# Loading each block of the second expert table as two 64-partition DMAs, one begun by SyncE and one by ScalarE

## The chip, the cores and the metric

The kernel runs on one core of one Trainium2 chip. Its engines are TensorE (PE), VectorE (DVE), ScalarE (ACT), GpSimd (POOL) and SyncE (SP); SP computes nothing here and begins DMAs. ACT and POOL also begin DMAs, and the profile shows the transfers of SP on queue q1, those of ACT on queue q10 and those of POOL on queue q0. All of them are carried by the core's 16 DMA engines. The metric is the device time of one execution in microseconds; shorter is better.

## The reference, cut to what matters

One layer of a hybrid encoder on 384 tokens (256 of a prompt, 128 of running streams), all in float32:

```
proj = rmsnorm(x) @ w_in                     # pool branch, q, k, v
h = x + concat(pool_mixer, diff_attention) @ w_out
xn = rmsnorm(h)
# PEER: 8 heads choose 16 of 16384 experts for each token
s = (xn @ w_pq) against sub_keys;  eidx, g = the 16 best of 128 x 128 pairs, softmax over them
a = gelu(u_tab[eidx] . xn)                   # u_tab is 16384 x 2048 float32, 134 MB
y = h + sum_k (g * a)[k] * v_tab[eidx[k]]    # v_tab is 16384 x 2048 float32, 134 MB
```

The outputs are y and the new keys, values and pooling rows. The change touches only the last line: how v_tab comes into the chip.

## The kernel before, in words

The layer is computed in stages. In the profiled execution the projections, attention and the output product fill the first 660 us, the query product and the search for the best keys most of what comes before 860 us, the stage of the first table (u) runs from there to about 1870 us, and the stage of the second table (v) from there to the end.

**The v stage.** v_tab is read once and whole, as 128 blocks of 128 experts (`v_v`, line 299: partition p of block m holds row 128 p + m, which is 8 KB). For the first 256 tokens y is a dense product: for each block, TensorE multiplies a 128 x 256 matrix of weights (gate times activation, mostly zero) with the 128 x 2048 block. A float32 product of full precision is made of three: each operand is split in a rounded part "hi" and a rest "lo", and `three` (lines 1296 to 1299) issues hi.hi, hi.lo, lo.hi. A block is 24 matmuls of 128 x 512 (`v_step`). The sums stay in the eight PSUM banks through all blocks.

For each block m the steps are:

- SP loads the block, 1 MB, into one of four buffers `vraw[m % 4]` (`v_weights`, line 375), once the lo part of block m - 4 has been made from that buffer (the wait on `lo_done` at line 412).
- ACT waits for the block (`v_in`) and writes its hi part, `v_hi`, line 814. After the even blocks it also writes the hi part of the weights of two blocks, `w_hi`, line 819.
- DVE writes the lo part, line 1257, and signals `lo_done`. After the lo part of an even block it multiplies the gates and activations of two blocks (`w_product`, line 1221), after that of an odd block it writes the lo part of the weights (`w_lo`, line 1226), for which it waits on the `w_hi` that ACT issues behind the hi part of the next, even block.
- SP also loads the dense gates and activations, 2 times 256 KB for two blocks (`v_routes`, line 379), on the same queue.

The names `v_raw` and `raw` in the profile are the buffers of blocks 0 and 1 and of blocks 2 and 3 (modulo 4); their hi parts are `ring_hi` and `v_hi`, their lo parts `ring_lo` and `v_lo`.

Beside this, the last 128 tokens are done without the product. For each of their 128 choices, POOL gathers the 128 rows of v_tab that the tokens chose, 1 MB in 8 KB rows, into one of five buffers (`gather_row`, line 529), and DVE adds them into `h` with their weights (`add_row`, line 1240). POOL waits with a gather until DVE has used the row that lay in its buffer. Before every eighth row POOL also gathers 8 columns of activations, one number a partition (`gather_gelus`, line 537). These adds stand in DVE's program between the lo parts, about 1.05 of them a block.

Every engine follows its own program in the order written; nothing is scheduled at run time. A wait in ACT's program holds up all that ACT does behind it.

**The u stage**, which is not changed, matters because it moves its blocks in a similar way: each 1 MB block of u_tab comes in eight DMAs of 32 partitions with runs of 2 KB (`u_piece`, line 301). SP begins the four pieces of partitions 0 to 31 and 64 to 95 (line 349), ACT the four of partitions 96 to 127 and 32 to 63 (`u_upper`, line 774). Before that, the w_pq blocks come in four pieces of 32 partitions, all from SP (line 344), while w_in and w_out blocks come in four DMAs of 128 partitions (line 327). All of these have runs of 2 KB.

Of the kernel before, what the change touches and what calls it, by code (L numbers as in the profile page):

```python
# [21 lines left out]
P = 128  # L22
# [24 lines left out]
BASE_V = BASE_U + P  # L47
# [32 lines left out]
VS = 4  # L80
# [41 lines left out]
def hybrid_layer(nc, I, O):  # L122
    F32, F32R, U32 = mybir.dt.float32, mybir.dt.float32r, mybir.dt.uint32
    ALU, ACT, AX = mybir.AluOpType, mybir.ActivationFunctionType, mybir.AxisListType
    ds = bass.ds
    ctx = ExitStack()
    with ctx:
# [6 lines left out]
        def at(name, kb, shape, dt=F32):  # L134
            return nc.alloc_sbuf_tensor_at(name, shape, dt, offset=base + int(kb * KB))
# [100 lines left out]
        vraw = [at("v_raw0", WK + 32, [P, D])[:, :], at("v_raw1", WK + 40, [P, D])[:, :], raw[:, 0, :], raw[:, 1, :]]  # L236
# [15 lines left out]
        def sem(n):  # L252
            names[n] = ctx.enter_context(nc.semaphore(n))
            return names[n]
# [5 lines left out]
        hi_done, lo_done, split_used = sem("hi_done"), sem("lo_done"), sem("split_used")  # L260
# [21 lines left out]
        v_in = [sem(f"v_in{i}") for i in range(VS)]  # L282
# [16 lines left out]
        v_v = I["v_tab"][0].rearrange("(p q) d -> p q d", q=P)  # L299

        def u_piece(m, k, a, h):

            return (raw[32 * a:32 * a + 32, k, 2 * h * W:2 * (h + 1) * W].rearrange("p (q r d) -> p q r d", r=2, q=1),
                    u_v[a, :, ds(m, 1), 2 * h:2 * h + 2, :])

        def wait_block(eng, t, blk, n_last):

            if t < NT - 1:
                eng.wait_ge(proj_ready, blk * 2 + (t + 1))
            else:  # L310
                eng.wait_ge(split_used, n_last + 3)
# [7 lines left out]
        def _(sp):  # L319
# [36 lines left out]
            def stored_gelu(mp, k):  # L356

                sp.wait_ge(a_store[k], mp * 16 + 16)
                sp.sem_inc(a_free, 1)
# [14 lines left out]

            def v_weights(m, slot):

                sp.dma_start(vraw[slot], v_v[:, ds(m, 1), :].rearrange("p o d -> p (o d)")).then_inc(v_in[slot], 16)

            def v_routes(j, par):

                sp.dma_start(gt[:, par, :, :], Gd[ds(j * 2, 2), :, :].rearrange("q p t -> p q t")).then_inc(ag_in[par], 16)
                sp.dma_start(at_[:, par, :, :], Ad[ds(j * 2, 2), :, 0:TD].rearrange("q p t -> p q t")).then_inc(ag_in[par], 16)

            sp.wait_ge(rt_ready, NT)
            v_weights(0, 0)
            v_weights(1, 1)
            sp.wait_ge(dot_done, DOTS)
            stored_gelu(P // 2 - 3, 1)
            store_gelu(P - 4, 0)
# [3 lines left out]
            v_routes(0, 0)  # L393
            sp.wait_ge(u_turn, P + 1)
            v_weights(2, 2)
            sp.wait_ge(u_turn, P + 2)
            v_weights(3, 3)
            v_routes(1, 1)
            stored_gelu(P // 2 - 2, 1)
            store_gelu(P - 2, 0)  # L400
# [5 lines left out]
            with sp.Fori(1, P // VS) as it:  # L406
                for par in range(2):
                    sp.wait_ge(w_mult, it * 2 + (par - 1))
                    v_routes(it * 2 + par, par)
                    for q in range(2):  # L410
                        s = 2 * par + q
# [150 lines left out]
        def _(act):  # L562
# [50 lines left out]
            with act.Fori(0, NG) as g:  # L613
                def evac_block(blk, tiles=range(NT)):
                    dst = qk[:, blk, :, :] if blk < 2 else vs[:, :, :]
                    for t in tiles:
                        wait_block(act, t, g * 3 + blk, g * 12 + (4 * blk + 3))
                        A(dst[:, t, :], bank[t][:, :], ACT.Copy).then_inc(proj_free, 1)

                for s in range(SPLIT, 12):  # L620
                    split_hi(g * 12 + s, s % 2)
                    m = s // 4 - 1
# [97 lines left out]
            for t in range(NT):  # L720
                wait_block(act, t, 9, BASE_POOL + 3)
                A(ptok[:, t, :], bank[t][:, :], ACT.Copy).then_inc(proj_free, 1)
# [90 lines left out]

            def v_hi(m, s, sets):

                act.wait_ge(v_in[s], sets * 16 + 16)
                A(vH[s], vraw[s], ACT.Copy).then_inc(hi_done, 1)

            def w_hi(j, par):

                act.wait_ge(w_mult, j + 1)
                A(wth[:, par, :, :], wt[:, par, :, :], ACT.Copy).then_inc(wh_done, 1)

            act.wait_ge(split_used, BASE_V + 1)
            v_hi(0, 0, 0)
            w_hi(0, 0)
            act.wait_ge(split_used, BASE_V + 2)
            v_hi(1, 1, 0)
            v_hi(2, 2, 0)
            w_hi(1, 1)  # L830
            v_hi(3, 3, 0)
            with act.Fori(1, P // VS) as it:
                for s in range(VS):
                    act.wait_ge(split_used, it * VS + (s + BASE_V - 1))
                    v_hi(it * VS + s, s, it)
                    if s % 2 == 0:
                        act.wait_ge(split_used, it * VS + (s + BASE_V))
                        w_hi(it * 2 + s // 2, s // 2)


        @block.vector
        def _(dve):
# [241 lines left out]
            def add_residual(nb, tiles=range(NT)):  # L1084
                for t in tiles:
                    wait_block(dve, t, 10 + nb, BASE_WOUT + 4 * nb + 3)
                    hs = hh[:, t, nb * W:(nb + 1) * W]
                    V.tensor_tensor(hs, bank[t][:, :], hs, ALU.add).then_inc(h_done, 1)
# [496 lines left out]
```

## Time and profile before

| | us |
|---|---|
| median of 3 runs | 2655.49 (2642.95 to 2659.84) |
| the profiled execution, its own time | 2656.08 |
| its span, first to last instruction | 2654.5 |
| PE busy | 2437.1 (92% of the span) |
| DVE busy | 1922.1 (72%) |
| POOL busy | 1171.8 (44%) |
| ACT busy | 932.1 (35%) |

How the rows below are read. A row of **windows** gives the stretch in us from the span's start and its length, the busy us and instruction counts of PE, PE's weight loads, DVE, ACT and POOL, then TensorE's granted clock as a share of full speed, the busy share of the 16 DMA engines, and GB/s moved. An answer on the **DMAs** of a stretch has packets, MB and mean rate; then for each queue its packets, its MB, and the time of its packets as a share of 16 engines times the stretch; then the issues, with the KB of each and the median us from issue to landing. Its row GB/s cuts the stretch in 40 equal slices. A **waits** row reads: who waited, for whom, us in all, how often, the longest. A **timeline** row has start, duration (both us), engine, line and operation, and in brackets the idle time before and what ended it. A row of a **tile** or a line gives counts, the least, median and longest duration in ns, and the first and last start in us.

### The profile page before, as it was taken

What the parts mean: (1) busy time and instruction counts of PE and PEld (TensorE: products, weight loads), DVE (VectorE), ACT (ScalarE), POOL (GpSimd) and SP (SyncE); (2) the same over time, 40 slices, a digit from 0 to 9 for tenths busy, and PEclk for the clock granted to TensorE, in tenths of its full rate; (3) what the DMA queues carried; (4) which work ended last, traced back from release to release, by engine and by line L of the source; (5) the groups of instructions that cost most, each with busy time, mean ns of one, the idle gap of its engine ahead of it and who ended that gap; (6) DMA issues with size and microseconds to landing.
All of it is one profiled execution on the core that took longest, in us unless ns stands there. A gap on an engine that the chain in (4) does not pass through costs nothing.

```text
span 2654.5 us, 38865 instructions
## 1 busy us (share of the span) xinstructions
PE 2437.1 (92%) x13838; PEld 2178.1 (82%) x13838; DVE 1922.1 (72%) x2105; ACT 932.1 (35%) x1018; POOL 1171.8 (44%) x684
## 2 busy tenths in 40 slices
PE   5989999999799999999979898898998999999899
PEld 4878777788699999999979898898776777777777
DVE  4554654643567998989877776776588898888888
ACT  3354544522333333323322232222333333333333
POOL 1020101020000010177888888882676675767662
PEclk9999999999899999999989999998999999999999
DMA  5453544495355568689888998997899999999997
GB/s 184 132 186 112 174 129 135 150 380 190 81 119 122 163 199 224 183 230 220 212 235 231 264 245 231 237 241 202 304 390 390 399 385 411 387 391 406 394 398 301
DMA packets 280169, 661.43 MB, mean 249 GB/s; under 512 B 73145, under 2 KB 123129, under 8 KB 237912
## 3 DMA queue, kind: packets, MB, share of 16 engines
q1 hardware_dynamic: 154832, 334.57, 38.9%
q0 software_dynamic: 82064, 249.26, 27.7%
q10 hardware_dynamic: 43191, 76.58, 10.2%
q8 instruction: 43, 0.70, 0.1%
q14 instruction: 39, 0.31, 0.0%
HBM read 613.65 MB, written 46.02 MB: 249 GB/s over the span
## 4 chain that ended last, share of the span: by engine, by line
PE 36%; POOL 25%; DMA 15%; DVE 13%; issue 7%; DVEq 1%; ACT 1%; ACTq 1%; SPq 0%; POOLq 0%
POOL g_dense L500 16%; PE banks L1297 11%; PE banks L1298 11%; PE banks L1299 11%; POOL a_values L542 6%; DMA a_tile<-a_dense 4%; DVE h L1249 4%; DMA v_row<-in_v_tab,route_place 3%; DMA raw<-in_v_tab 3%; POOL u_row L494 2%; DMA v_raw<-in_v_tab 2%; DMA raw<-in_u_tab 2%; POOL v_row L533 1%; DVEq L847 1%; DVE u_turned L1126 1%
## 5 line engine op out<-in xcount | busy, mean ns | idle before, releaser
L1297 PE MATMUL banks<-xT_hi,ring_hi 128*128 128x320 f32 (+1 forms) x2304 | 737.2, 320 | 88.4 <-DVE ring_lo L1130 81.2
L1298 PE MATMUL banks<-xT_lo,ring_hi 128*128 128x320 f32 (+1 forms) x2304 | 731.3, 317 | 0.0
L1299 PE MATMUL banks<-xT_hi,ring_lo 128*128 128x320 f32 (+1 forms) x2304 | 730.8, 317 | 0.0
L500 POOL DMA_INDIRECT g_dense<-route,route_place x256 | 497.1, 1942 | 132.1 <-issue 76.2
L1297 PEld LDWEIGHTS banks<-xT_hi,ring_hi 128*128 128x128 f32 x2304 | 444.8, 193 | 98.6 <-issue 83.3
L1298 PEld LDWEIGHTS banks<-xT_lo,ring_hi 128*128 128x128 f32 x2304 | 444.9, 193 | 0.0
L1299 PEld LDWEIGHTS banks<-xT_hi,ring_lo 128*128 128x128 f32 x2304 | 444.1, 193 | 0.0
L533 POOL DMA_INDIRECT v_row<-in_v_tab,route_place x128 | 284.4, 2222 | 187.3 <-DVE h L1249 165.4
L868 DVE TENSOR_TENSOR ring_lo<-raw,ring_hi 128x2048 fp32r<-128x2048 f32 x72 | 164.8, 2292 | 252.7 <-ACT ring_hi L580 252.4
L1130 DVE TENSOR_TENSOR ring_lo<-u_turned,ring_hi 128x2048 fp32r<-128x2048 f32 x128 | 290.5, 2270 | 72.3 <-ACT ring_hi L785 71.8
L1126 DVE STREAM_TRANSPOSE u_turned<-raw 128x2048 f32<-128x2048 f32 x128 | 295.6, 2310 | 63.7 <-DMA raw<-in_u_tab 55.5
L1249 DVE SCALAR_TENSOR_TENSOR h<-v_row,w_values,h 128x2048 f32<-128x2048 f32 x128 | 300.5, 2348 | 38.8 <-DMA v_row<-in_v_tab,route_place 36.1
L785 ACT ACTIVATE ring_hi<-u_turned 128x2048 fp32r<-128x2048 f32 x128 | 245.3, 1916 | 233.5 <-issue 220.7
L542 POOL DMA_INDIRECT a_values<-a_dense,route_place x128 | 232.5, 1817 | 60.6 <-issue 38.7
L1297 PE MATMUL banks<-v_hi,w_hi 128*128 128x512 f32 x512 | 204.3, 399 | 30.2 <-DVE v_lo L1257 30.1
L1297 PE MATMUL banks<-ring_hi,w_hi 128*128 128x512 f32 x512 | 205.1, 401 | 27.6 <-DVE ring_lo L1257 27.4
L791 ACT ACTIVATE gelu_out<-banks 128x320 f32<-128x320 f32 x128 | 56.0, 437 | 494.9 <-PE banks L1299 494.9
L580 ACT ACTIVATE ring_hi<-raw 128x2048 fp32r<-128x2048 f32 x72 | 137.6, 1914 | 214.3 <-PE banks L1299 167.0
L1298 PE MATMUL banks<-ring_lo,w_hi 128*128 128x512 f32 x512 | 203.0, 397 | 0.0
L1299 PE MATMUL banks<-ring_hi,w_lo 128*128 128x512 f32 x512 | 202.9, 396 | 0.0
L1298 PE MATMUL banks<-v_lo,w_hi 128*128 128x512 f32 x512 | 201.9, 394 | 0.0
L1299 PE MATMUL banks<-v_hi,w_lo 128*128 128x512 f32 x512 | 201.6, 394 | 0.0
(219 smaller groups left out, 3791.6 us busy)
## 6 DMA issues: line engine op xcount, KB each, us to landing
raw<-in_u_tab SPq DMA_DIRECT2D x512, 128.0 KB
raw<-in_u_tab ACTq DMA_DIRECT2D x512, 128.0 KB
v_raw<-in_v_tab SPq DMA_DIRECT2D x64, 1024.0 KB, 10.8
raw<-in_v_tab SPq DMA_DIRECT2D x64, 1024.0 KB, 12.1
raw<-in_w_in SPq DMA_DIRECT2D x160, 256.0 KB
a_dense<-gelu_out SPq DMA_DIRECT2D x128, 160.0 KB
raw<-in_w_out SPq DMA_DIRECT2D x64, 256.0 KB
g_dense<-zeros POOLq DMA_DIRECT2D x16, 1024.0 KB, 28.9
```

Of the source, the lines that this page charges most:

```text
L500: pool.indirect_dma_start(out=places, out_offset=bass.IndirectOffsetOnAxis(ap=routeU[:, t, 2, j:j + 1], axis=0), in_=route[:, t, 0, j:j + ...
L533: pool.indirect_dma_start(out=vrow[k % NVB][:, :], out_offset=None, in_=rows, in_offset=bass.IndirectOffsetOnAxis(ap=routeU[:, NT - 1, 1, ...
L542: pool.indirect_dma_start(out=aval[0:P - GT, k:k + 1], out_offset=None, in_=gelus, in_offset=bass.IndirectOffsetOnAxis(ap=routeU[0:P - GT, ...
L580: A(ringH[:, slot, :], raw[:, slot, :], ACT.Copy).then_inc(hi_done, 1)
L785: A(ringH[:, k, :].rearrange("p (b r i) -> p r b i", b=KC, r=4), uT[:, k, :].rearrange("p (r b i) -> p r b i", r=4, b=KC), ACT.Copy).then_ ...
L868: V.tensor_tensor(ringL[:, slot, :], raw[:, slot, :], ringH[:, slot, :].bitcast(F32), ALU.subtract).then_inc(lo_done, 1)
L1126: V.transpose(uT[:, k, :], raw[:, k, :]).then_inc(u_turn, 1)
L1130: V.tensor_tensor(ringL[:, k, :].rearrange("p (b r i) -> p r b i", b=KC, r=4), uT[:, k, :].rearrange("p (r b i) -> p r b i", r=4, b=KC), r ...
L1249: V.scalar_tensor_tensor(out=acc, in0=vrow[k % NVB][:, :], scalar=wval[:, k:k + 1], in1=acc, op0=ALU.mult, op1=ALU.add).then_inc(row_used, 1)
L1297: MM(out, h1, h2, start=first, stop=False)
L1298: MM(out, h1, l2, start=False, stop=False)
L1299: return MM(out, l1, h2, start=False, stop=last)
```

## The change

Each block of v_tab is loaded by two DMAs, partitions 0 to 63 and partitions 64 to 127, each 512 KB in 64 rows of 8 KB. `v_half` names the two sides.

- For blocks 0 to 3 SP begins both halves, one behind the other.
- For blocks 4 to 127 SP begins the lower half where it began the whole block, under the same wait. ACT begins the upper half of block m + 3 right behind the hi part of block m (`v_next`), and waits before it for the same count of `lo_done` as SP: the lo part of block m - 1.
- The hi part waits for both halves (the count for one set of four buffers is 32 in place of 16).
- The loop on ACT is the same otherwise; its last turn is written out, because only block 127 is left to load there.

```
+        def v_half(m, slot, half):
+            part = slice(64 * half, 64 * half + 64)
+            return vraw[slot][part, :], v_v[part, ds(m, 1), :].rearrange("p o d -> p (o d)")
...
             def v_weights(m, slot):
-                sp.dma_start(vraw[slot], v_v[:, ds(m, 1), :].rearrange("p o d -> p (o d)")).then_inc(v_in[slot], 16)
+                sp.dma_start(*v_half(m, slot, 0)).then_inc(v_in[slot], 16)
+            def v_upper(m, slot):
+                sp.dma_start(*v_half(m, slot, 1)).then_inc(v_in[slot], 16)
...
             v_weights(0, 0)
+            v_upper(0, 0)
...
             def v_hi(m, s, sets):
-                act.wait_ge(v_in[s], sets * 16 + 16)
+                act.wait_ge(v_in[s], sets * 32 + 32)
                 A(vH[s], vraw[s], ACT.Copy).then_inc(hi_done, 1)
...
+            def v_next(m, slot):
+                act.wait_ge(lo_done, m + (BASE_V - 1))
+                act.dma_start(*v_half(m, slot, 1)).then_inc(v_in[slot], 16)
+
+            def v_set(it, loads=VS):
+                for s in range(VS):
+                    act.wait_ge(split_used, it * VS + (s + BASE_V - 1))
+                    v_hi(it * VS + s, s, it)
+                    if s < loads:
+                        v_next(it * VS + (s + VS - 1), (s + VS - 1) % VS)
+                    if s % 2 == 0:
+                        act.wait_ge(split_used, it * VS + (s + BASE_V))
+                        w_hi(it * 2 + s // 2, s // 2)
...
             v_hi(1, 1, 0)
+            v_next(4, 0)
             v_hi(2, 2, 0)
+            v_next(5, 1)
             w_hi(1, 1)
             v_hi(3, 3, 0)
-            with act.Fori(1, P // VS) as it:
-                for s in range(VS):
-                    act.wait_ge(split_used, it * VS + (s + BASE_V - 1))
-                    v_hi(it * VS + s, s, it)
-                    if s % 2 == 0:
-                        act.wait_ge(split_used, it * VS + (s + BASE_V))
-                        w_hi(it * 2 + s // 2, s // 2)
+            v_next(6, 2)
+            with act.Fori(1, P // VS - 1) as it:
+                v_set(it)
+            v_set(P // VS - 1, 1)
```

ACT's program in the loop over blocks, before. One turn of the loop treats four blocks; the rows are the first two of them and the start of the third (`ring_hi` and `v_hi_119` are the hi parts, `w_hi` that of the weights; `v_in` counts the landed blocks, `split_used` the steps that TensorE has done, `w_mult` the products of DVE):

```order
L816 ISA [waits split_used]
L817 ACTIVATE ring_hi<-v_raw_117 128x2048 [waits v_in0]
L837 REGISTER_ALU
L821 ISA [waits split_used]
L822 ACTIVATE w_hi<-w_tile 128x512 [waits w_mult]
L817 ACTIVATE ring_hi<-v_raw_118 128x2048 [waits v_in1,split_used]
L834 REGISTER_ALU
L817 ACTIVATE v_hi_119<-raw 128x2048 [waits v_in2,split_used]
```

The same place in the changed kernel:

```order
L829 ISA [waits split_used]
L830 ACTIVATE ring_hi<-v_raw_117 128x2048 [waits v_in0]
L840 REGISTER_ALU
L841 ISA [waits lo_done]
L841 DMA raw<-in_v_tab 64x2048
L851 REGISTER_ALU
L834 ISA [waits split_used]
L835 ACTIVATE w_hi<-w_tile 128x512 [waits w_mult]
L830 ACTIVATE ring_hi<-v_raw_118 128x2048 [waits v_in1,split_used]
L840 REGISTER_ALU
L841 ISA [waits lo_done]
L841 DMA v_raw_117<-in_v_tab 64x2048
```

A wait on DVE's lo part and a DMA now stand behind each hi part; behind the hi parts of the even blocks they stand ahead of `w_hi`.

SP's program at the same place, before (the loads of the first two blocks of four; the routes of the next two stand behind them):

```order
L412 ISA
L377 ISA [waits lo_done]
L377 DMA v_raw_117<-in_v_tab 128x2048
L412 REGISTER_ALU
L377 ISA [waits lo_done]
L377 DMA v_raw_118<-in_v_tab 128x2048
L381 ISA [waits w_mult]
L381 DMA g_tile<-g_dense 128x2x256
```

and now:

```order
L425 ISA
L382 ISA [waits lo_done]
L382 DMA v_raw_117<-in_v_tab 64x2048
L425 REGISTER_ALU
L382 ISA [waits lo_done]
L382 DMA v_raw_118<-in_v_tab 64x2048
L390 ISA [waits w_mult]
L390 DMA g_tile<-g_dense 128x2x256
```

The order on SP is the same; each DMA of a block has half its partitions, and the routes have half a block less ahead of them in their queue for each block.

## Rows read from the trace of the kernel before

**Rows 1.** Windows: first part of the v stage, the rest, its steady middle.
```profile
1870.00:1960.00 90.00, 81.39 (x349) 66.40 (x348) 67.55 (x45) 38.15 (x28) 69.83 (x38) 0.96 0.90 344
1960.00:2640.00 680.00, 630.80 (x2685) 511.16 (x2684) 586.12 (x356) 242.28 (x166) 446.10 (x217) 0.98 0.99 391
2000.00:2600.00 600.00, 552.61 (x2350) 447.33 (x2349) 511.80 (x312) 213.90 (x147) 406.97 (x199) 0.97 1.00 396
```

**Rows 2.** DMAs from 2000 to 2600 us, the steady middle of the v stage.
```profile
DMA packets 58864, 237.37 MB, mean 396 GB/s; under 512 B 7878, under 2 KB 33040, under 8 KB 33040
...
q1 hardware_dynamic: 40859, 128.62, 56.0%
q0 software_dynamic: 17999, 108.70, 44.2%
...
raw<-in_v_tab SPq DMA_DIRECT2D x50, 1024.0 KB, 12.5
```

**Rows 3.** DMAs from 2200 to 2300 us, GB/s in slices of 2.5 us.
```profile
GB/s 409 416 426 407 362 392 410 422 387 410 432 419 412 409 395 413 423 425 394 418 408 419 416 372 412 387 400 154 154 366 431 426 423 423 423 419 420 405 417 414
```

**Rows 4.** Waits from 2000 to 2600 us, of ACT on its blocks and of DVE.
```profile
ACT v_hi L817 <- DMA raw<-in_v_tab: 167.9, 41, 13.9
...
DVE w_tile L1224 <- DMA a_tile<-a_dense: 39.4, 14, 5.8
...
DVE h L1249 <- DMA v_row<-in_v_tab,route_place: 26.4, 9, 5.7
...
DVE w_lo L1229 <- ACT w_hi L822: 20.2, 11, 2.3
```

**Rows 5.** Timeline of TensorE in the v stage: the same matmul of two successive threes.
```profile
2187.04 0.39 PE L1297 MATMUL banks<-v_hi,w_hi 128*128 128x512 f32 x1
...
2187.72 0.39 PE L1297 MATMUL banks<-v_hi,w_hi 128*128 128x512 f32 x1
```

**Rows 6.** Timeline of ACT, DVE and SP over two blocks without a gap on DVE.
```profile
2217.89 1.92 ACT L817 ACTIVATE v_hi<-raw 128x2048 fp32r<-128x2048 f32 x1 [2.28 <-DMA raw<-in_v_tab]
...
2219.71 0.61 ACT L822 ACTIVATE w_hi<-w_tile 128x512 fp32r<-128x512 f32 x1
2220.47 2.28 DVE L1257 TENSOR_TENSOR ring_lo<-v_raw,ring_hi 128x2048 fp32r<-128x2048 f32 x1
...
2222.67 0.68 DVE L1229 TENSOR_TENSOR w_lo<-w_tile,w_hi 128x512 fp32r<-128x512 f32 x1
...
2225.53 2.28 DVE L1257 TENSOR_TENSOR v_lo<-raw,v_hi 128x2048 fp32r<-128x2048 f32 x1
...
2227.99 0.35 SPq L377 DMA_DIRECT2D raw<-in_v_tab  x1
```

**Rows 7.** The DMA issues of ACT in the u stage, line 778.
```profile
L778 ACTq DMA_DIRECT2D raw<-in_u_tab x512: 317/448/1168, 827.4 to 1842.9; - x171
```

**Rows 8.** DMAs from 230 to 260 us: w_in, 128 partitions.
```profile
q1 hardware_dynamic: 1884, 3.44, 36.7%
```

**Rows 9.** DMAs from 585 to 640 us: w_out, 128 partitions, beside POOL's stores.
```profile
q1 hardware_dynamic: 4449, 8.10, 42.9%
```

**Rows 10.** DMAs from 720 to 740 us: w_pq, 32 partitions, all from SP.
```profile
GB/s 98 188 164 139 143 131 168 172 172 131 119 176 160 193 98 25 0 70 115 168 168 193 168 148 197 180 168 168 168 180 8 0 0 0 29 123 147 180 172 160
...
q1 hardware_dynamic: 1365, 2.50, 60.1%
```

**Rows 11.** DMAs from 900 to 960 us: u_tab, 32 partitions; ACT's queue.
```profile
q10 hardware_dynamic: 2560, 4.20, 24.9%
```

**Rows 12.** DMAs from 984 to 1004 us: u_tab pieces beside POOL's 8 KB rows.
```profile
DMA packets 2050, 5.94 MB, mean 297 GB/s; under 512 B 344, under 2 KB 533, under 8 KB 1629
...
q0 software_dynamic: 468, 3.44, 54.8%
```

**Rows 13.** First four loads of v_raw, and who used them, 1842 to 1880 us.
```profile
L377 SPq DMA_DIRECT2D v_raw<-in_v_tab x4: 345/353/473, 1842.8 to 1879.5; - x4
L817 ACT ACTIVATE ring_hi<-v_raw x2: 1898/1900/1902, 1871.2 to 1873.5; 128x2048 fp32r<-128x2048 f32 x2
```

More of the change, by code:

```diff
@@ L385, in _ @@
             v_weights(0, 0)
+            v_upper(0, 0)
             v_weights(1, 1)
+            v_upper(1, 1)
             sp.wait_ge(dot_done, DOTS)
@@ L395, in _ @@
             v_weights(2, 2)
+            v_upper(2, 2)
             sp.wait_ge(u_turn, P + 2)
             v_weights(3, 3)
+            v_upper(3, 3)
             v_routes(1, 1)
```

## The prediction

> **What bounds the kernel now.** The diff touches only the v stage, so I read the windows of that stage first [rows 1]. From 2000 to 2600 us TensorE issues 2350 matmuls, 24 to a block: 98 blocks in 600 us, 6.12 us a block. Three resources are near that. TensorE: the same matmul of two successive threes starts 0.68 us apart [rows 5], so 24 need 8 x 0.68 = 5.44 us. DVE: 511.8 us of work over 98 blocks is 5.22 us a block [rows 1]. The DMA engines: their busy share is 1.00 at 396 GB/s [rows 1]. So the DMAs are the bound.
>
> The waits agree [rows 4]. ACT waits 167.9 us for the blocks of `raw` alone, which costs nothing by itself (it works 214 of 600 us), but DVE's idle time, 600 - 511.8 = 88 us, is nearly all there as well: 39.4 us for the activations' tile, 26.4 us for gathered rows, 20.2 us for `w_hi`, which itself waits behind the hi part of a block that has not landed.
>
> How near to their limit are the DMA engines? In slices of 2.5 us the rate is 405 to 426 GB/s most of the time and falls to 154 for two slices [rows 3]. A typical full slice is 423. A block moves 237.37 / 98 = 2.42 MB [rows 2]: 1.05 MB of v_tab, 108.70 / 98 = 1.11 MB in POOL's queue (a gathered row and more) and 0.26 MB of routes. The two queues' shares, 56.0% and 44.2%, fill the engines [rows 2]. A block therefore costs 1.002 x 9600 / 98 = 98 us of one engine's time, which over 16 engines is the 6.12 us.
>
> **The change, part by part.**
>
> *Number and size of the pieces.* The runs stay 8 KB and the bytes stay the same. SP's issues stay one a block in the loop; 124 new issues stand on ACT. An issue keeps ACT 0.32 to 0.45 us [rows 7], 0.45 x 124 = 56 us on an engine that idles over 60% here: nothing by itself, what it holds up comes below. For blocks 0 to 3 SP issues four more, 0.35 us each; the first block is begun at 1842.8 and first used at 1871.2 [rows 13], so 28 us of cover hide them. Without the cover they would cost 1.4 us.
>
> *How well half blocks move.* The trace of before has no 64-partition loads with 8 KB runs, but it has the same question at 32 partitions, all with runs of 2 KB. Time of one engine per MB: w_in, 128 partitions, 0.367 x 480 / 3.44 = 51.2 us [rows 8]; w_out, 128 partitions, 0.429 x 880 / 8.10 = 46.6 us [rows 9]; w_pq, pieces of 32 partitions one after the other on SP's queue, 0.601 x 320 / 2.50 = 76.9 us, and its rate stays at 168 to 197 GB/s at best [rows 10]; u_tab, pieces of 32 partitions begun by SP on one side and ACT on the other, 0.249 x 960 / 4.20 = 56.9 us on ACT's queue [rows 11]. So a transfer that reaches only a part of the partitions is dearer, by 50% against w_in when its complement is not beside it, by 11% when SP and ACT bring both sides at about the same time. The change is of the second kind: both engines wait for the same lo part. Its price for the half blocks lies between nothing and 50%; I take the 11% of the u_tab row, which it is nearest to. At the 39.0 us per MB that POOL's queue pays in the v stage (0.442 x 9600 / 108.70, [rows 2]) a block of v_tab costs 1.05 x 39.0 = 40.9 us of one engine, and 11% of it over 16 engines is **0.28 us a block**; at 50% it would be 1.28 us.
>
> The neighbours may pay too. Beside the u_tab pieces, POOL's 8 KB rows cost 0.548 x 320 / 3.44 = 51.0 us per MB and the whole moves 297 GB/s [rows 12], against 39.0 us and 396 GB/s in the v stage [rows 2]. That is 31% more for the same kind of rows. If the split caused all of it, 1.11 x 39.0 x 0.31 / 16 = 0.84 us a block would come on top; if the runs of 2 KB did, nothing. I take a quarter, **0.21 us**, since half blocks keep the long runs and that is the larger difference between the two stretches.
>
> The Trainium skill has the reason for such a price (SBUF — State Buffer, Door 1: The DMA port swizzle): partitions 0 to 63 reach only 8 of the 16 ports through which DMAs write. The w_pq row agrees with it. By its figures, two half transfers side by side run only 6% above the 196 GB/s of one (same page, "Can I just issue two DMAs to hit both halves?"); the estimate from that is 1.05 / 0.208 + 1.37 / 0.396 = 8.5 us a block, and the u_tab row speaks against so much.
>
> *The new wait on ACT.* ACT now waits for the lo part of block m - 1 behind the hi part of block m, and begins a DMA, before it goes on. The next hi part is not held up: its block lands later anyway [rows 4]. But behind an even block stands `w_hi`, and DVE wants that right behind the lo part of block m - 1. In the rows over two blocks, `w_hi` started at 2219.71, while the lo part of the block before ran from 2220.47 to 2222.75 and `w_lo` followed at 2222.67 without a gap [rows 6]. In the changed order: lo part done at 2222.75, its signal reaches the next engine 0.18 us later (2225.53 + 2.28 to SP's issue at 2227.99), the issue takes 0.45 [rows 7], `w_hi` 0.61, then `w_lo`: 2224.0 in place of 2222.67. DVE stands still for about 1.35 us every two blocks, 0.68 us a block. DVE then needs 5.22 + 0.68 = 5.90 us a block, less than the 6.12 + 0.49 = 6.61 of the DMAs, with 0.71 us left for its other waits (39.4 + 26.4 us, 0.67 a block). So I cost it at nothing while the DMAs are the bound: time that DVE stands still is time in which late blocks and rows catch up. Without that cover it costs 0.68 us a block. Between 1870 and 1960 us the DMAs are not yet the bound (share 0.90, 349 matmuls, 14.5 blocks, [rows 1]) and TensorE's 5.44 us is: there DVE's 5.90 makes 0.46 x 14.5 = **6 us**.
>
> *Turns between queues.* Three queues now share the engines. The v blocks and routes get more of the turns, the gathered rows fewer. No bytes are saved, so while the engines are full it shifts who waits for whom; its gain is the last rival.
>
> **The sum.** From 1960 to 2640 us there are 2685 / 24 = 112 blocks [rows 1]. 112 x 0.49 = 55 us, and 6 us: +61 us on the profiled execution's own 2656.1, which stands 0.6 us above the median of the runs. That gives **2716 us**, 2.3% slower.
>
> **The rivals.**
>
> *No change, 2656 us (2632 to 2682).* Half blocks with long runs from two queues may mix so well that both sides are always busy, and DVE's wait is absorbed. For it: the engines run at 396 GB/s because of bytes, which do not change. Against it: every row of part-wise loads in the trace is dearer than its whole-width neighbour. The Trainium skill predicts this outcome as well (DMA: Bandwidth & Descriptors, Rules for kernel authors): of two transfers to disjoint halves it says "Don't bother", since both run on the same 16 engines. Chance 0.28.
>
> *The wait on ACT is not absorbed, 2760 to 2830 us.* DVE's waits for rows and activations may stay as they are, because POOL begins a gather only when DVE has used a row: a late DVE makes late rows. Then 0.68 us comes on top of the DMAs' term, 112 x 0.68 = 76 us, 2792 us. For it: a DVE without gaps is what catches up after each dip [rows 3, 6], and it loses that reserve. Against it: a queue that is full delays everybody less when somebody comes later. Chance 0.12.
>
> *The halves get in each other's way, 2830 to 2925 us.* Priced by the dear rows: 1.28 + 0.84 = 2.12 us a block, 237 + 6 us, 2899 us. The page's 8.5 us a block gives 2924. For it: w_pq [rows 10]; and both halves have the same three queues' turns on all engines, so that many engines may write the same side at once. Against it: u_tab's row, with both sides under way, is far from that price. Chance 0.10.
>
> *Faster, 2612 us.* The routes lie behind half as many bytes in SP's queue, and v blocks land sooner. If that removed the dips, so that the engines ran at 423 GB/s all the time, 237.37 MB would take 561 us in place of 600, times 680 / 600: 44 us less. It decides if DVE's 39.4 us for the activations vanish [rows 4] and no price of the halves appears. Against it: a dip comes when all four v blocks have landed and POOL is at its small gathers, and blocks that land sooner make it longer; and rows, which DVE also waits for, get fewer turns. Chance 0.10.
>
> **How the numbers follow.** The forecast, 2682 to 2760 us, has 0.40. About 1% (27 us) is what a measurement of this kernel can tell from no change, its three runs lying within 17 us. Faster by over 1%: 0.10. Within: 0.28. Slower: 0.40 + 0.12 + 0.10 = 0.62. The range takes in forecast, no change and the unabsorbed wait, and the near end of the dear halves, since their price is the least certain term: 2632 to 2850. The forecast's own is 2682 to 2760.
>
> **What would show it.** Steady windows of the v stage: DMA share still about 1.00, and GB/s down from 396 to about 367 (2.42 / 6.61). If GB/s stays at 396, the price of the halves was wrong. The cost per MB on ACT's new queue should be near 43 us, and on POOL's a little above 39.0. In the waits, `w_lo` behind `w_hi` should rise from 11 times to nearly every second block, at about 1.3 us, and DVE's waits for rows and activations should shrink; if they do not, the wait is not absorbed. A rate above 396 together with shorter waits for the activations would make the faster rival right.

## The result, and the profile after

The change takes 3033.3 us (median of 4 runs, 3005.8 to 3061.3) against 2654.0 us before: a ratio of 1.1395, 95% interval 1.1348 to 1.1442. The forecast was 2716 us with a range up to 2850. The direction was right and the size was not: 379 us in place of 62. The profiled execution has a span of 3021.9 us, against 2654.5 before. Each ratio in this document compares fast executions with those of the kernel before that were measured beside them; the slow ones that the ratios leave out are the 3061.3 us here and one of 8371.7 us among the four of run 1.

The windows of the v stage, which answer to [rows 1] (same columns; the steady stretch is longer now, since the stage ends near 3000 us):

```profile
1870.00:1960.00 90.00, 68.23 (x254) 54.07 (x255) 47.69 (x32) 24.01 (x17) 47.57 (x34) 0.83 1.00 248
...
2000.00:2600.00 600.00, 416.91 (x1629) 330.50 (x1628) 352.72 (x213) 146.48 (x101) 271.81 (x143) 0.84 1.02 268
```

1629 matmuls are 67.9 blocks in 600 us: 8.84 us a block in place of 6.12. The DMA engines are as full as before, 1.02, but move 268 GB/s in place of 396. That is the core of the result in two numbers: the engines' time per byte went up by half. 112 blocks at 2.72 us more are 305 of the 367 us between the two profiled executions. The first 90 us, where TensorE was the bound, do 10.6 blocks in place of 14.5, and the engines are full there too; 3.9 blocks at 8.84 us are 35 us. The remaining 27 us are not taken apart further; towards the end the blocks are a little slower, 9.0 us each from 2600 to 2950 us.

TensorE is busy for only 417 of the 600 us now, and its granted clock is 0.84 in place of 0.97. It waits for lo parts, which wait for blocks, so it follows the DMAs and does not set the time:

```profile
PE banks L1325 <- DVE ring_lo L1285: 104.1, 16, 15.8
```

The DMAs from 2000 to 2600 us, which answer to [rows 2] (packets, MB, share of 16 engines; then issues, KB each and median us to landing):

```profile
DMA packets 41149, 160.75 MB, mean 268 GB/s; under 512 B 6635, under 2 KB 23659, under 8 KB 23659
...
q0 software_dynamic: 12369, 73.30, 43.2%
q1 hardware_dynamic: 23371, 52.02, 35.2%
q10 hardware_dynamic: 5406, 35.40, 23.3%
...
raw<-in_v_tab SPq DMA_DIRECT2D x34, 512.0 KB, 11.5
raw<-in_v_tab ACTq DMA_DIRECT2D x34, 512.0 KB, 25.1
...
a_tile<-a_dense SPq DMA_DIRECT2D x34, 256.0 KB, 29.0
```

ACT's queue q10 carries nothing but upper halves: 0.233 x 9600 / 35.40 = 63.2 us of one engine per MB. The prediction had 43. POOL's rows on q0, which the change does not touch, cost 0.432 x 9600 / 73.30 = 56.6 us per MB against 39.0. So the halves are dear and make their neighbours nearly as dear. The upper half lands after 25 or 26 us, the lower after 11.

The waits of DVE and ACT from 2000 to 2600 us, which answer to [rows 4] (us in all, times, longest):

```profile
ACT v_hi L830 <- DMA raw<-in_v_tab: 187.8, 17, 22.3
DVE w_tile L1252 <- DMA a_tile<-a_dense: 175.8, 17, 16.2
...
DVE w_lo L1257 <- ACT w_hi L835: 54.5, 32, 3.4
```

DVE's wait for the activations' tile is up from 39.4 to 175.8 us. The tile lies in SP's queue as before; it takes 29.0 us from issue to landing in place of 14.9, since all that the engines carry has become slower.

The new wait on ACT is there as well, in the timeline of the changed kernel (start, duration, engine, line; idle time in brackets), which answers to [rows 6]:

```profile
2301.69 2.28 DVE L1285 TENSOR_TENSOR ring_lo<-v_raw,ring_hi 128x2048 fp32r<-128x2048 f32 x1
2305.44 0.69 DVE L1257 TENSOR_TENSOR w_lo<-w_tile,w_hi 128x512 fp32r<-128x512 f32 x1 [1.47 <-ACT w_hi L835]
```

`w_lo`, which followed the lo part without a gap, now comes 1.47 us after its end. The working out gave 1.35. Over the 600 us it waits 32 times, for nearly every pair of blocks, and 54.5 / 32 = 1.70 us each.

### The profile page after: what moved, and what is told of

It is laid out like the page before. It is cut to its first block, busy times and chain, and to the rows that moved or that the text cites. A ratio compares the mean times of both kernels' runs of the same rounds, so it can differ in the third digit from the quotient of the medians.

```text
span 3021.9 us, 39319 instructions
## 1 busy us (share of the span) xinstructions
PE 2507.9 (83%) x13838; PEld 2220.6 (73%) x13838; DVE 1927.0 (64%) x2105; ACT 931.9 (31%) x1018; POOL 1139.5 (38%) x684
## 4 chain that ended last, share of the span: by engine, by line
PE 30%; DMA 29%; POOL 17%; DVE 13%; issue 5%; ACT 1%; SPq 1%; DVEq 1%; ACTq 1%; POOLq 0%
DMA a_tile<-a_dense 24%; POOL g_dense L513 14%; PE banks L1325 9%; PE banks L1327 9%; PE banks L1326 9%; DVE h L1277 4%; POOL u_row L507 2%; DMA v_row<-in_v_tab,route_place 2%; DVE ring_lo L1285 2%; POOL a_values L555 2%; DVE u_turned L1154 1%; DVEq L875 1%; DMA raw<-in_u_tab 1%; DMA g_dense<-route,route_place 1%; DVE ring_lo L1158 1%
## 5 line engine op out<-in xcount | busy, mean ns | idle before, releaser
L546 POOL DMA_INDIRECT v_row<-in_v_tab,route_place x128 | 304.7, 2381 | 576.3 <-DVE h L1277 564.7
L1325 PE MATMUL banks<-ring_hi,w_hi 128*128 128x512 f32 x512 | 224.7, 439 | 222.2 <-DVE ring_lo L1285 222.1
L1325 PE MATMUL banks<-v_hi,w_hi 128*128 128x512 f32 x512 | 216.6, 423 | 133.5 <-DVE v_lo L1285 133.3
L1325 PEld LDWEIGHTS banks<-ring_hi,w_hi 128*128 128x128 f32 x512 | 108.2, 211 | 260.7 <-DVE ring_lo L1285 231.5
L1252 DVE TENSOR_TENSOR w_tile<-a_tile,g_tile 128x512 f32<-128x512 f32 x64 | 44.1, 689 | 343.0 <-DMA a_tile<-a_dense 342.9
L830 ACT ACTIVATE v_hi<-raw 128x2048 fp32r<-128x2048 f32 x64 | 122.2, 1910 | 409.5 <-DMA raw<-in_v_tab 382.1
L1325 PEld LDWEIGHTS banks<-v_hi,w_hi 128*128 128x128 f32 x512 | 104.2, 203 | 167.9 <-DVE v_lo L1285 145.8
L830 ACT ACTIVATE ring_hi<-v_raw 128x2048 fp32r<-128x2048 f32 x64 | 122.4, 1912 | 331.6 <-DMA v_raw<-in_v_tab 253.5
L1326 PE MATMUL banks<-ring_lo,w_hi 128*128 128x512 f32 x512 | 218.4, 427 | 0.0
L1327 PE MATMUL banks<-ring_hi,w_lo 128*128 128x512 f32 x512 | 216.1, 422 | 0.0
```

What stands on the lines that cost most here:

```text
L546: pool.indirect_dma_start(out=vrow[k % NVB][:, :], out_offset=None, in_=rows, in_offset=bass.IndirectOffsetOnAxis(ap=routeU[:, NT - 1, 1, ...
L1325: MM(out, h1, h2, start=first, stop=False)
L1326: MM(out, h1, l2, start=False, stop=False)
L1327: return MM(out, l1, h2, start=False, stop=last)
```

## The experiments

The theory after the result: a DMA that writes partitions of one half only costs the engines about half as much again per byte, and what runs beside it pays too. Its rivals: the third queue and how the engines share their turns; ACT's wait and issues; the number or size of the DMAs; the place in HBM that a half reads.

**1. Both halves from SP.** No third queue, ACT as before.

```
-                sp.dma_start(vraw[slot], v_v[:, ds(m, 1), :]...).then_inc(v_in[slot], 16)
+                for half in range(2):
+                    part = slice(64 * half, 64 * half + 64)
+                    sp.dma_start(vraw[slot][part, :], v_v[part, ds(m, 1), :]...).then_inc(v_in[slot], 16)
```

> Both halves of every block are begun by SP, one behind the other, where the whole block was begun; ACT's program is that of before. If the width of the transfers is what costs (each MB of a 64-partition transfer takes about 1.5 times the engine time, and its neighbours pay too), this stays far slower than before: 2900 to 3100 us, with the v stage at 250 to 300 GB/s and a DMA share of 1.0. If the third queue or ACT's wait is the cause, both are gone and the time is 2655 to 2680 us at 390 GB/s or more.

3085.5 us, ratio 1.162 (1.157 to 1.167). Its DMAs from 2000 to 2600 us:

```profile
DMA packets 39022, 152.31 MB, mean 254 GB/s; under 512 B 6160, under 2 KB 22473, under 8 KB 22473
...
q0 software_dynamic: 11586, 69.39, 44.5%
```

254 GB/s, and POOL's rows at 61.6 us per MB. The whole price is there with two queues and without ACT. Beginning the halves from two engines makes it a little smaller (1.14), not larger.

**2. Two DMAs by columns.** Same issues and waits as the change, but each DMA covers all partitions.

```
-            part = slice(64 * half, 64 * half + 64)
-            return vraw[slot][part, :], v_v[part, ds(m, 1), :]...
+            cols = slice(1024 * half, 1024 * half + 1024)
+            return vraw[slot][:, cols], v_v[:, ds(m, 1), cols]...
```

> The two DMAs of a block are now its left and its right 1024 columns, each over all 128 partitions with runs of 4 KB; SP begins the one, ACT the other, with the waits of the change. If the width is what costs, this is near before: 2655 to 2700 us, 380 to 400 GB/s. If three queues sharing the engines cost, or ACT's wait, it is as slow as the change, about 3000 us.

2682.9 us, ratio 1.0115 (1.0068 to 1.0161). From 2000 to 2600 us:

```profile
DMA packets 69515, 226.57 MB, mean 378 GB/s; under 512 B 9136, under 2 KB 32809, under 8 KB 56837
...
q10 hardware_dynamic: 13546, 49.33, 20.7%
```

40.3 us per MB on ACT's queue. With three queues, the wait and twice the issues, but full width, 1.2% of the 14% are left. The engines are at a share of 0.98 here, so they are no longer quite full. The activations' tile lands after 11.8 us in place of 14.9 and DVE waits 32.7 us for it in place of 39.4, and still the kernel is no faster.

**3. Swapped sides.** SP begins partitions 64 to 127, ACT 0 to 63 (`part = slice(64 - 64 * half, 128 - 64 * half)`).

> As the change, but SP begins partitions 64 to 127 and ACT partitions 0 to 63. The time should be that of the change, 3000 to 3060 us. In the change SP's half lands in 11 us and ACT's in 25 us. If that goes by the queue, ACT's half is the late one here too (25 us); if it goes by the side of the memory that is written, SP's half is now the late one.

3036.8 us, one run. Issues from 2000 to 2600 us:

```profile
raw<-in_v_tab SPq DMA_DIRECT2D x32, 512.0 KB, 23.9
raw<-in_v_tab ACTq DMA_DIRECT2D x32, 512.0 KB, 11.9
```

The cost does not depend on who begins which half. The late half is now SP's, so lateness does not go by the queue.

**4. ACT's wait alone.** Whole blocks from SP; `v_next` keeps its wait and begins nothing.

> The blocks are loaded whole by SP as before; only ACT's wait for the lo part of the block before stands where the change put it, with no DMA behind it. If the wait is absorbed while the DMA engines are full, 2650 to 2680 us, with w_lo waiting for w_hi in nearly every second block for about 0.9 us (1.35 less the issue). If it is not absorbed: 112 x 0.45 us, 2705 us. If it carried most of the change's 379 us, 2900 us or more.

2644.2 us (7 runs), ratio 0.9962 (0.9945 to 0.9979): the kernel is 0.4% faster than before. Waits of DVE and the windows' row from 2000 to 2600 us:

```profile
DVE w_lo L1252 <- ACT w_hi L831: 49.3, 50, 2.3
DVE w_tile L1247 <- DMA a_tile<-a_dense: 24.7, 13, 3.6
DVE h L1272 <- DMA v_row<-in_v_tab,route_place: 3.6, 3, 1.6
```

```profile
2000.00:2600.00 600.00, 562.42 (x2374) 449.83 (x2374) 520.01 (x315) 215.28 (x148) 404.71 (x200) 0.98 1.01 399
```

The bare wait costs nothing; the issue that follows it in the change is not part of this run. `w_lo` waits 50 times, 0.99 us each (0.9 expected), but the waits for the tile and the rows fall from 39.4 and 26.4 to 24.7 and 3.6 us: 77.6 us of waits in all against 86.0. So it is absorbed by the waits that the prediction named. Why there is a gain on top, no run takes apart. This is the fastest version of the study, ahead of both kernels.

**5. Even and odd partitions.** 64 partitions to a DMA as in the change, but every second one.

```
+            return vraw[slot][half::2, :], v_v[half::2, ds(m, 1), :]...
```

> As the change, 64 partitions to a DMA, but SP begins the even partitions and ACT the odd ones, so that each DMA reaches both sides of the memory. If it is the side (a DMA of partitions 0 to 63 or 64 to 127 writes through half of the ports), the cost goes away: 2655 to 2720 us and more than 370 GB/s. If it is that a DMA of 64 partitions gives each engine other partitions than a DMA of 128 does, it stays: 2900 us or more.

2689.8 us, ratio 1.013 (1.0099 to 1.0162). From 2000 to 2600 us, first the queues, then DVE's wait:

```profile
DMA packets 57586, 225.38 MB, mean 376 GB/s; under 512 B 9100, under 2 KB 33078, under 8 KB 33078
...
q10 hardware_dynamic: 7511, 49.29, 20.1%
```

```profile
DVE w_lo L1256 <- ACT w_hi L834: 67.8, 45, 1.5
```

39.1 us per MB on ACT's queue: the same number of partitions, of DMAs, of runs of 8 KB, of queues as in the change, and the price is gone. So it is not the count of 64 partitions but which partitions they are. All the dear DMAs of this study write a contiguous range inside one half, all the cheap ones write both halves evenly; a contiguous range across the middle, 32 to 95, was not tried, so that it is the half and not the contiguous range is not shown by a run. The wait is 1.51 us each, with the issue in it, and the engines' share is 0.97.

**6. Crossed source.** Partitions 0 to 63 read what belongs to 64 to 127, and the other way round (`v_v[other, ...]`).

> As the change, but partitions 0 to 63 are loaded from the table rows of partitions 64 to 127 and the other way round; the bytes and issues are the same, and the dense product uses the wrong rows, so y of the first 256 tokens is not the reference's. About 3030 us in any case. In the change and in its swapped form the DMA of partitions 64 to 127 lands late (24 to 28 us against 11 to 12). If that is the side of the memory written, ACT's half (partitions 64 to 127, first half of the table) stays the late one; if it is the place in HBM, SP's half is late now.

3042.1 us, one run. Issues from 2000 to 2600 us:

```profile
raw<-in_v_tab ACTq DMA_DIRECT2D x34, 512.0 KB, 11.7
raw<-in_v_tab SPq DMA_DIRECT2D x34, 512.0 KB, 21.6
```

The cost is that of the change. The late half follows the table's second half here, not the partitions. That made the place read in HBM a rival for the whole cost, since in the change each half also reads one half of the table; runs 9 and 10 part the two.

**7. Half the dose.** Blocks 0 and 1 of four in halves, 2 and 3 whole (`if slot < 2` before the halves).

> Blocks 0 and 1 of every four come in halves as in the change, blocks 2 and 3 whole from SP; all of ACT's waits stay. If the price is paid for each MB moved in halves, half of the 379 us: 2820 to 2870 us. If two streams of halves must meet to cost, or the engines lose step with each other once disturbed, it is nearer one of the ends: under 2750 or over 2950 us.

2853.2 us, ratio 1.076 (1.0722 to 1.0797): 200 us of the 379, 53%. From 2000 to 2600 us:

```profile
q0 software_dynamic: 14723, 86.75, 42.5%
q10 hardware_dynamic: 3200, 20.97, 14.1%
```

The price is paid for each MB moved in halves; POOL's rows cost 47.0 us per MB, between 39.0 and 56.6.

**8. Routes on ACT's queue.** Whole blocks from SP, ACT's wait, and ACT begins the route tiles of blocks 8 to 127 behind `w_hi`.

```
+                        if loads == VS:
+                            j, par = it * 2 + (s // 2 + 2), s // 2
+                            act.dma_start(gt[:, par, :, :], Gd[ds(j * 2, 2), :, :]...).then_inc(ag_in[par], 16)
+                            act.dma_start(at_[:, par, :, :], Ad[ds(j * 2, 2), :, 0:TD]...).then_inc(ag_in[par], 16)
```

> A version meant to beat both: whole blocks from SP, ACT's wait for the lo part as in the version with the wait alone (0.4% faster than before), and the route tiles of blocks 8 to 127 begun by ACT behind w_hi on its own queue, where they lie behind no block. If DVE's waits for the activations' tile (39.4 us of 600 before) were from lying behind blocks in SP's queue, 2610 to 2640 us; if full engines set the time, 2640 to 2655 us.

2679.4 us, ratio 1.0091 (1.0065 to 1.0117): slower, neither expectation. Its DVE wait and issues from 2000 to 2600 us:

```profile
DVE w_tile L1258 <- DMA a_tile<-a_dense: 60.7, 14, 8.0
```

```profile
a_tile<-a_dense ACTq DMA_DIRECT2D x47, 256.0 KB, 15.5
```

The tile lands no sooner than from SP's queue (median 15.5 against 15.3 us in run 4), though it is begun no later: a median of 5.4 us after DVE's last product, against 6.1 us in run 4. What differs is the spread, the latest landing after 24.1 us against 18.9. The wait for the tile grew from 24.7 to 60.7 us; why the tile lands so unevenly is open.

**9 and 10. Source and destination parted.** Run 9 writes halves and reads every second row; run 10 writes every second partition and reads halves.

```
run 9:   return vraw[slot][part, :],    v_v[half::2, ds(m, 1), :]...
run 10:  return vraw[slot][half::2, :], v_v[part, ds(m, 1), :]...
```

> Destination as in the change (SP writes partitions 0 to 63, ACT 64 to 127), but SP reads every second of the 128 table rows of a block, so that each DMA reads from both halves of the table; the dense product gets wrong rows, so y of the first 256 tokens is not the reference's. If the side of the memory that is written carries the cost, about 3030 us and 265 GB/s, as the change. If the half of the table that is read carries it (the late DMA of the last runs followed the table's second half, not the partitions), 2660 to 2720 us.

> The mirror of it: SP writes the even partitions and ACT the odd ones, but SP reads the rows of the table's first half and ACT those of its second; y of the first 256 tokens is not the reference's. If the side written carries the cost, 2660 to 2720 us; if the half of the table that is read does, about 3030 us. If both forms cost something, each has a share.

Run 9: 3058.2 us; run 10: 2680.3 us; one run each. From 2000 to 2500 us, run 9:

```profile
DMA packets 33272, 130.24 MB, mean 260 GB/s; under 512 B 5285, under 2 KB 19105, under 8 KB 19105
...
q10 hardware_dynamic: 4313, 28.26, 21.9%
```

and run 10:

```profile
DMA packets 48067, 188.18 MB, mean 376 GB/s; under 512 B 7615, under 2 KB 27599, under 8 KB 27599
...
q10 hardware_dynamic: 6240, 40.90, 19.8%
```

62.0 against 38.7 us per MB (share x 8000 / MB). The partitions that are written carry the cost, the half of the table that is read carries none.

**11. Even and odd, both from SP.** Run 1's edit with `half::2` for `part`.

> Even and odd partitions as two DMAs, both begun by SP one behind the other; no third queue, no wait on ACT. If the 1.3% that the even and odd form still cost came from the third queue and ACT's part, this is before's time, 2640 to 2665 us. If it came from the number of DMAs or their size, 2680 to 2700 us.

2664.9 us, ratio 1.0055 (1.0037 to 1.0074). Of the 1.3% of run 5, 0.55% stay with two DMAs from SP; the other part goes with ACT's queue, wait and issues. Run 4 shows that it is not the bare wait; whether it is the third queue or the issue ahead of `w_hi` is open.

**12 and 13. Without POOL.** The gathers of rows and activations and DVE's adds are left out, first in the change, then in the kernel before.

> The change with POOL's gathers of rows and of activations and DVE's adds left out, so y of the last 128 tokens lacks the expert part. The v stage then moves 1.31 MB a block in place of 2.42. If the halves are dear by themselves, their packets cost about 63 us of an engine per MB as in the change, the engines still are not full (1.31 MB at 63 us per MB is 5.2 us a block over 16 engines, TensorE needs 5.44), and the v stage takes 5.5 to 5.9 us a block: 2530 to 2590 us. If the cost needs POOL's rows beside them, 40 to 45 us per MB on ACT's queue.

> The kernel before with POOL's gathers and DVE's adds left out, so y of the last 128 tokens lacks the expert part: whole blocks and routes only. The control of the same cut of the change, where halves cost 68 us of an engine per MB with nothing of POOL beside them and the engines were full at 237 GB/s. If halves are dear by themselves, whole blocks cost 37 to 45 us per MB here, the engines are 60 to 70% busy at 240 GB/s, and TensorE bounds it: 2560 to 2585 us. If a block costs over 60 us per MB here too, the high number there is only what a DMA with time to spare shows.

2582.9 us and 2579.2 us, one run each: nearly no difference, because TensorE is the bound (2192 and 2208 matmuls in 500 us, 5.47 and 5.43 us a block). The DMAs from 2000 to 2500 us tell it, the change's first:

```profile
DMA packets 39153, 118.26 MB, mean 237 GB/s; under 512 B 4340, under 2 KB 27630, under 8 KB 27630
...
q1 hardware_dynamic: 31967, 71.19, 63.6%
q10 hardware_dynamic: 7185, 47.07, 40.2%
```

and before's:

```profile
DMA packets 38279, 120.61 MB, mean 241 GB/s; under 512 B 2946, under 2 KB 26502, under 8 KB 26502
...
q1 hardware_dynamic: 38278, 120.60, 68.0%
```

1.038 x 8000 / 118.26 = 70.2 us of an engine per MB with halves, 45.1 with whole blocks: 56% more, with no POOL traffic beside them. The halves are dear by themselves. ACT's queue alone pays 0.402 x 8000 / 47.07 = 68.3 us per MB, more than the 63 expected, so the engines are full against expectation. They are full at 237 GB/s, which is just what TensorE asks for (241 with whole blocks), which is why so little shows in the time. The same halves cost 14% where the engines were the bound and 0.1% where they were not.

**14. Quarters, in the order of the u stage.**

```
+            return [(vraw[slot][32 * a:32 * a + 32, :], v_v[32 * a:32 * a + 32, ds(m, 1), :]...)
+                    for a in ((0, 2), (3, 1))[half]]
```

> Each block in four DMAs of 32 partitions, in the order of the u stage: SP begins 0 to 31 and then 64 to 95, ACT 96 to 127 and then 32 to 63. If it is enough that the sides alternate at short distance, on each queue and between the two, under 2800 us and over 330 GB/s. If every DMA that writes one side only is dear, whatever comes behind it, 2950 us or more and 250 to 290 GB/s; then the u stage, which is loaded so, pays the same price.

3023.7 us, one run. From 2000 to 2500 us:

```profile
DMA packets 35842, 132.97 MB, mean 266 GB/s; under 512 B 7146, under 2 KB 21397, under 8 KB 21397
...
q10 hardware_dynamic: 5245, 28.69, 22.9%
```

63.9 us per MB: the price of the halves. Alternating the sides on each queue does not help. The other half of the expectation, that the u stage pays the same, is taken up below.

## Why the prediction was wrong

- **What bounds the kernel: right.** The v stage was bound by full DMA engines, and it still is (share 1.02).
- **The failed step: the price of half blocks.** The text took "the 11% of the u_tab row, which it is nearest to", 0.28 us a block, and a quarter of the neighbours' 0.84 us, together 0.49 us. Measured are 2.72 us. The upper halves cost 63.2 us per MB where 39.0 was the base, 62% more, beyond even the upper end of 50%; the neighbours cost 45% more, not 8%. The dear rival, 2.12 us a block and 2899 us, had the mechanism at nearly its size and got a chance of 0.10; even it was 134 us short.
- **Outside the steady stretch.** For the first 90 us the text counted only DVE's new gap, 0.46 x 14.5, which is 6.7 us and not 6. It took the DMAs to have room there; with the dear halves they are full, and 35 us are lost.
- **Why the wrong row was taken.** The u_tab row comes from 900 to 960 us, where the two queues fill 34.8% and 24.9% of the engines. [rows 12] come from a stretch with full engines, like the v stage, and said 297 GB/s. The queues of the same u_tab pieces in that stretch, in the kernel before:

```profile
q1 hardware_dynamic: 839, 1.27, 24.0%
q10 hardware_dynamic: 742, 1.22, 23.9%
```

  That is 0.240 x 320 / 1.27 = 60.5 and 0.239 x 320 / 1.22 = 62.7 us per MB, against 56.9 in the row that was taken: nearly the 63.2 that the halves came to cost, and it stood in the trace of before. Had the v stage's 2.42 MB been priced at 297 GB/s, a block would have cost 8.15 us and the kernel 2656 + 112 x 2.03 + 6 = 2889 us. The text put three quarters of that row down to its runs of 2 KB. Run 14 shows 32-partition pieces with runs of 8 KB at 63.9 us per MB and 266 GB/s: short runs are not needed for the price. The reading that SP's and ACT's pieces complement each other was wrong too: run 1, from one queue, costs 16%, the change 14%.
- **The cause the text named fits the runs.** The price goes by the partitions that each DMA writes (runs 1, 5, 9, 10). The Trainium skill says that partitions 0 to 63 reach only 8 of the 16 ports (SBUF — State Buffer, Door 1: The DMA port swizzle); by its map the even partitions alone reach all 16. The runs agree, 39.1 us per MB for even or odd partitions and 63.2 for a half, but none of them shows the ports themselves.
- **A near estimate, in part by luck.** The estimate by the Trainium skill's figures (SBUF — State Buffer, "Can I just issue two DMAs to hit both halves?"), 8.5 us a block, was the nearest of all to the measured 8.84. It has 5.05 us for the block's own bytes and 3.46 for the rest. The runs divide it otherwise: by the queues' shares, upper halves took 0.233 x 600 / 67.9 = 2.06 us a block, so both halves, taken as alike, about 4.1, and the rest 4.9.
- **The rival of no change: its reading was wrong.** The Trainium skill's rule (DMA: Bandwidth & Descriptors, Rules for kernel authors) follows "Don't bother" with the words that the two transfers serialize and the advice to use one of 128 partitions. The text read it as a forecast of no change, which it does not state; the change costs 14%.
- **The wait on ACT: right in the main.** 1.35 us expected, 1.47 us in the timeline after, 1.70 us in the mean of the change and 1.51 us in run 5. The bare wait is absorbed while the DMAs are the bound, as run 4 shows (0.9962). With the issue in it, it is one candidate for the 1.2 to 1.3% of runs 2 and 5, where the engines' share is 0.98 and 0.97. The sign that the text gave, shrinking waits for rows and activations, came true in run 4 (26.4 to 3.6 and 39.4 to 24.7 us); in the change the wait for activations rose to 175.8 us, because of the halves.
- **The turns between queues: small, as said.** In the kernels in which ACT begins DMAs that write both halves (runs 2, 5, 8) the whole cost is 0.9 to 1.3%, with ACT's wait and issues in it. The faster rival falls with run 2: the price of the halves is gone and the tile comes sooner (11.8 against 14.9 us), but the rate is 378 GB/s and not 423.
- **The first blocks and the issues: right at nothing**, as far as run 11's 0.55% allows, which the text had not counted for twice as many DMAs.

## What to carry to other kernels

When the DMA engines are near full, keep a transfer whole; if it must be split, split it by columns or by every second partition, and not into a lower and an upper half. Look at the engines' time per MB (share x 16 x stretch / MB), which shows the price even where another engine hides it. And take the price of a resource from a row where that resource is as busy as it will be: the same u_tab pieces cost 56.9 us per MB at 60% load and 62.7 with the engines full, beside POOL's rows. A ratio needs the same care. The 11% were against w_in's 51.2 us with runs of 2 KB; the block that was replaced cost 39.0 with runs of 8 KB, and 63.2 is 62% above that.

## What the runs showed of the hardware

- DMAs of 64 partitions all in one half cost 62 to 65 us of an engine per MB beside other traffic (ACT's queue: 63.2 in the change, 64.5 in run 7, 62.0 in run 9), those of 64 even or odd ones 39 us (runs 5 and 10), 32-partition pieces with runs of 8 KB 64 us (run 14).
- The price spreads to whatever shares the engines: POOL's untouched rows went from 39.0 to 56.6 us per MB, and to 47.0 with half of the blocks in halves.
- One half lands after 11 to 12 us and the other after 22 to 28, although both are begun in the same moment. Over the change, run 3 and run 6 the late one was that with the table's second half, in either partitions and on either queue; in run 9, where each DMA read both halves of the table, it was still late on partitions 64 to 127 (25.9 against 11.6 us for `raw`, but only 14.2 against 10.1 for `v_raw`). What decides it stays open; the total did not depend on it (3033 to 3058 us).
- Why ACT's wait alone makes the kernel 0.4% faster is open as well.
